# Expert weights in transfers of two slabs (2 MB, 16 KB runs), with the ring of 20 slabs handled as 10 groups

## The reference

```python
logits = t @ w_router + b_router              # 256 tokens, 32 experts, the best 4 of each token
up = xb @ w_up[e] + b_up[e]                   # w_up[e]: 1024 x 2048, 8 MB
glu, lin = up[:, :D_FF_EXPERT], up[:, D_FF_EXPERT:]
glu = jnp.minimum(glu, SWIGLU_LIMIT)
lin = jnp.clip(lin, -SWIGLU_LIMIT, SWIGLU_LIMIT)
act = glu * jax.nn.sigmoid(SWIGLU_ALPHA * glu) * (lin + 1)
y = act @ w_down[e] + b_down[e]               # w_down[e]: 1024 x 1024, 4 MB
```

## Time and profile before

| | |
|---|---|
| Time, median of 3 runs | 1238.82 us (1234.84 to 1239.2) |
| The profiled execution's own time | 1234.07 us |
| Its span, first to last instruction | 1232.4 us |
| PE busy | 1152.1 us, 93% of the span |
| DVE, ACT, POOL busy | 330.0, 237.0, 85.7 us |
| Data moved | 436.22 MB, mean 354 GB/s over the span |
| DMA packets | 65135 |

### The profile page before, as it was taken

One profiled execution on the slowest core, in us unless ns is written; L12 is line 12 of the kernel. 1 busy time (PEld: TensorE's weight loads), 2 busy tenths in 40 slices (PEclk: granted clock), 3 DMA queues, 4 the chain that ended last, 5 costly groups with the idle time before them and its releaser, 6 DMA issues.

```text
span 1232.4 us, 17087 instructions
## 1 busy us (share of the span) xinstructions
PE 1152.1 (93%) x5306; PEld 497.6 (40%) x5307; DVE 330.0 (27%) x859; ACT 237.0 (19%) x453; POOL 85.7 (7%) x204
## 2 busy tenths in 40 slices
PE   6969999998999999999899999999989999899996
PEld 5757548653333333333333333333333333333332
DVE  1389631333211122221111232111111111111112
ACT  2214121321121111112111121121111111111112
POOL 1098000010000000000000000000000000000000
PEclk9989999999999999999999999999999999999999
DMA  9230643909999999999999999999999999999991
GB/s 354 93 145 3 271 171 137 370 22 394 422 421 421 421 422 422 421 421 422 421 422 422 421 422 422 421 422 421 421 404 422 421 422 422 391 422 422 421 398 46
DMA packets 65135, 436.22 MB, mean 354 GB/s; under 512 B 8019, under 2 KB 8190, under 8 KB 15934
## 3 DMA queue, kind: packets, MB, share of 16 engines
q1 hardware_dynamic: 65086, 435.68, 85.7%
HBM read 434.61 MB, written 1.05 MB: 354 GB/s over the span
## 4 chain that ended last, share of the span: by engine, by line
PE 47%; SPq 36%; issue 6%; DMA 5%; DVE 3%; ACT 2%; ACTq 0%; DVEq 0%
SPq L390 22%; PE bank L1476 14%; SPq L394 11%; PE bank L1490 8%; DMA ring<-in_w_up_dram 5%; PE total L1449 2%; PE bank L1436 2%; PE bank L1188 2%; PE bank L1361 2%; PE bank L1210 2%; DVE ring L903 1%; SPq L429 1%; SPq L428 1%; PE bank L1201 1%; PE total L1400 1%
## 5 line engine op out<-in xcount | busy, mean ns | idle before, releaser
L1476 PE MATMUL bank<-ring,buf_m 128*64 128x512 f32 x2112 | 474.1, 597 | 40.3 <-DMA ring<-in_w_up_dram 38.5
L1476 PEld LDWEIGHTS bank<-ring,buf_m 128*64 128x64 f32 x2112 | 145.7, 137 | 362.6 <-issue 263.7
L1490 PE MATMUL bank<-ring,buf_m 128*64 128x512 f32 x1056 | 239.5, 595 | 0.0
L1111 DVE COPY buf_f<-bank 128x512 f32<-128x512 f32 x33 | 22.8, 692 | 589.9 <-PE bank L1476 589.9
L1490 PEld LDWEIGHTS bank<-ring,buf_m 128*64 128x64 f32 x1056 | 72.8, 136 | 137.6 <-issue 129.2
L759 ACT ACTIVATE buf_f<-bank 128x512 f32<-128x512 f32 x33 | 19.7, 597 | 403.3 <-PE bank L1476 403.3
L1449 PE MATMUL total<-buf_m,wr_sb 64*128 64x512 f32 x272 | 67.6, 615 | 0.8 <-ACT buf_m L771 0.8
L1436 PE MATMUL bank<-buf_k,buf_v 128*64 128x512 f32 x272 | 65.9, 605 | 0.7 <-DVE buf_v L1062 0.7
L539 POOL TENSOR_TENSOR buf_v<-table,buf_v 128x4 f32<-128x4 f32 x33 | 6.6, 199 | 804.0 <-DVE buf_v L1099 803.7
L1117 DVE TENSOR_TENSOR buf_f<-bank,buf_v 128x512 f32<-128x512 f32 x66 | 45.4, 687 | 59.5 <-PE bank L1510 59.5
L756 ACT ACT_TABLE_LOAD x33 | 42.3, 1283 | 33.7 <-issue 33.7
(11 more groups left out here) (327 smaller groups left out, 915.8 us busy)
## 6 DMA issues: line engine op xcount, KB each, us to landing
ring<-in_w_up_dram SPq DMA_DIRECT2D x256, 1024.0 KB, 26.2
ring<-in_w_down_dram SPq DMA_DIRECT2D x128, 1024.0 KB, 26.4
ring<-in_w_in_dram SPq DMA_DIRECT2D x4, 1440.0 KB, 10.8
ring<-in_w_xkv_dram SPq DMA_DIRECT2D x2, 2048.0 KB, 24.3
ring<-in_w_xkv_dram SPq DMA_DIRECT2D x1, 4096.0 KB, 13.4
ring<-in_w_out_dram SPq DMA_DIRECT2D x1, 4096.0 KB, 14.1
ring<-in_w_xq_dram SPq DMA_DIRECT2D x2, 2048.0 KB, 21.1
ring<-in_w_xo_dram SPq DMA_DIRECT2D x1, 4096.0 KB, 12.8
```

The source lines that it names most:

```text
L1476: ins = t_.matmul(banks[c][h * 64:(h + 1) * 64, :], xg[:, k, :], w[:, h * FF + c * BANK:h * FF + (c + 1) * BANK], start=k == 0, stop=k == ...
L1490: ins = t_.matmul(banks[2][h * 64:(h + 1) * 64, :], actT[:, f, :], slab(slot_of(at))[:, k * D + h * BANK:k * D + (h + 1) * BANK], start=f ...
```

## The change

Two slabs make a group (`GROUP = 2`); the ring is 10 groups, and an expert takes 6 loads of 2 MB (4 of `w_up`, 2 of `w_down`) instead of 12 of 1 MB. The host now lays out `w_up` too so that a partition's share of one expert, 64 KB, is one piece in DRAM; a load takes 16 KB of it on each partition. (The address of a partition's run so lies 64 KB behind that of the partition before, where it was 8 KB; for `w_down` it is 32 KB before and after, with runs of 16 KB in place of 8 KB.) There is one semaphore per group. TensorE waits once for each group and raises `up_steps` and `down_steps` after the second slab of each; SyncE waits for these, so that a slot pair is free when both its slabs are used. In the trunk slab 3 of expert 1 (issued with the down slabs at about 166 us) and slab 0 of expert 1 (issued after `xs11`) move behind `gffn`, where four slabs of expert 1 now go out in two loads. What TensorE computes, and in which order, is the same.

```diff
-RING, SLABS, CYCLE = 20, 12, 5
+GROUP = 2
+UPS, DOWNS = 8 // GROUP, 4 // GROUP
+RING, LOADS, CYCLE = 20 // GROUP, 12 // GROUP, 5
...
-        up_v = w_up[0].rearrange("e (k p) n -> e p k n", p=P)
+        up_v = w_up
...
+        def group(slot):
+            return slab(slot * GROUP, GROUP)
+
+        WIDE = GROUP * SLAB
...
-            def load_up(e, at, k):
-                slot = slot_of(at + k)
-                sp.dma_start(slab(slot), up_v[e, :, k, :]).then_inc(slab_in[slot], 16)
+            def load_up(e, at, i):
+                slot = slot_of(at + i)
+                sp.dma_start(group(slot), up_v[e, :, i * WIDE:(i + 1) * WIDE]).then_inc(group_in[slot], 16)
...
-            for i in range(4):
+            for i in range(DOWNS):
                 load_down(0, 0, i)
-            load_up(1, SLABS, 3)
...
-            for k in range(4, KT):
-                load_up(0, 0, k)
-            wait_drained(sp, "xs11")
-            load_up(1, SLABS, 0)
+            load_up(0, 0, 2)
+            load_up(0, 0, 3)
             wait_drained(sp, "xv3")
-            for k in range(4):
-                load_up(0, 0, k)
+            load_up(0, 0, 0)
+            load_up(0, 0, 1)
             wait_drained(sp, "xo3")
             sp.dma_start(gffn, g_ffn[0:1, :].broadcast_to([P, D])).then_inc(loaded["gffn"], 16)
-            load_up(1, SLABS, 1)
-            load_up(1, SLABS, 2)
+            load_up(1, LOADS, 0)
+            load_up(1, LOADS, 1)
...
-                    for k in range(4):
-                        sp.wait_ge(up_steps, n2 * KT + (k + 5))
-                        load_up(e, j * SLABS, k)
-                    for k in range(4, KT):
-                        sp.wait_ge(down_steps, n2 * 4 + (k - 3))
-                        load_up(e, j * SLABS, k)
+                    for i in range(DOWNS):
+                        sp.wait_ge(up_steps, n2 * UPS + (DOWNS + i + 1))
+                        load_up(e, j * LOADS, i)
+                    for i in range(DOWNS, UPS):
+                        sp.wait_ge(down_steps, n2 * DOWNS + (i - DOWNS + 1))
+                        load_up(e, j * LOADS, i)
                     n1 = last_block(e - 1)
-                    for i in range(4):
-                        sp.wait_ge(up_steps, n1 * KT + (i + 1))
-                        load_down(e, j * SLABS, i)
+                    for i in range(DOWNS):
+                        sp.wait_ge(up_steps, n1 * UPS + (i + 1))
+                        load_down(e, j * LOADS, i)
...
+            def wait_loaded(turn, at):
+
+                pe.wait_ge(group_in[slot_of(at)], turn * (CYCLE * LOADS // RING * 16) + (at // RING + 1) * 16)
+
             def up_slabs(n, turn, j):
 
                 for k in range(KT):
-                    at = j * SLABS + k
-                    pe.wait_ge(slab_in[slot_of(at)], turn * (CYCLE * SLABS // RING * 16) + (at // RING + 1) * 16)
-                    w = slab(slot_of(at))
+                    i, part = divmod(k, GROUP)
+                    at = j * LOADS + i
+                    if part == 0:
+                        wait_loaded(turn, at)
+                    w = group(slot_of(at))[:, part * SLAB:(part + 1) * SLAB]
...
-                    ins.then_inc(up_steps, 1)
+                    if part == GROUP - 1:
+                        ins.then_inc(up_steps, 1)
...
+    inputs["w_up"] = np.asarray(inputs["w_up"])[0].reshape(E, KT, P, 2 * FF).transpose(0, 2, 1, 3).reshape(E, P, KT * 2 * FF)
```

More of the change, by code:

```diff
@@ L306, in build_program @@
         table_ready = sem("ranks_and_gates_in_table")
-        slab_in = [sem(f"slab{i}_in") for i in range(RING)]
+        group_in = [sem(f"slabs{i * GROUP}_to_{i * GROUP + GROUP - 1}_in") for i in range(RING)]
         p2_ready = sem("onehot_for_gather_ready")
@@ L386, in _ @@
                 sp.dma_start(wxq_sb[:, 4 * i:4 * i + 4, :], w_xq_v[:, 4 * i:4 * i + 4, :]).then_inc(loaded[f"wxq{i}"], 16)
-            def load_up(e, at, k):
-                slot = slot_of(at + k)
-                sp.dma_start(slab(slot), up_v[e, :, k, :]).then_inc(slab_in[slot], 16)
+            def load_up(e, at, i):
+                slot = slot_of(at + i)
+                sp.dma_start(group(slot), up_v[e, :, i * WIDE:(i + 1) * WIDE]).then_inc(group_in[slot], 16)
             def load_down(e, at, i):
-                slot = slot_of(at + KT + i)
-                sp.dma_start(slab(slot), down_v[e, :, i * SLAB:(i + 1) * SLAB]).then_inc(slab_in[slot], 16)
+                slot = slot_of(at + UPS + i)
+                sp.dma_start(group(slot), down_v[e, :, i * WIDE:(i + 1) * WIDE]).then_inc(group_in[slot], 16)
             wait_drained(sp, "oT1")
             sp.wait_ge(yconv_ready, 1)
-            for i in range(4):
+            for i in range(DOWNS):
                 load_down(0, 0, i)
-            load_up(1, SLABS, 3)
             wait_drained(sp, "w11")
@@ L418, in _ @@
                 sp.dma_start(y_sb[h * 64:h * 64 + E, :], b_down[0, :, h * BANK:(h + 1) * BANK]).then_inc(loaded["bdown"], 16)
-            for k in range(4, KT):
-                load_up(1, SLABS, k)
+            load_up(1, LOADS, 2)
+            load_up(1, LOADS, 3)
             sp.wait_ge(rows_ready, TT)
@@ L432, in _ @@
             n1 = last_block(0)
-            for i in range(4):
-                sp.wait_ge(up_steps, n1 * KT + (i + 1))
-                load_down(1, SLABS, i)
+            for i in range(DOWNS):
+                sp.wait_ge(up_steps, n1 * UPS + (i + 1))
+                load_down(1, LOADS, i)
             with sp.Fori(0, (E - 2) // CYCLE) as turn:
@@ L756, in _ @@
                     a.activation(scrap[:, 3:4], eps[:, 0:1], ACT.Sigmoid)
-                    act.wait_ge(up_steps, b * KT + KT)
+                    act.wait_ge(up_steps, b * UPS + UPS)
                     a.activation(U_sb[:, 0:BANK], banks[0], ACT.Copy).then_inc(u_by_a, 1)
@@ L768, in _ @@
                     gathered_columns(b + 1, 0)
-                    act.wait_ge(down_steps, b * 4 + 4)
+                    act.wait_ge(down_steps, b * DOWNS + DOWNS)
                     act.wait_ge(pt_copied, b + 2)
@@ L1109, in _ @@
                     onehot_for_gather(b + 1)
-                    dve.wait_ge(up_steps, b * KT + KT)
+                    dve.wait_ge(up_steps, b * UPS + UPS)
                     v.tensor_copy(U_sb[:, BANK:2 * BANK], banks[1]).then_inc(u_by_v, 1)
@@ L1478, in up_slabs @@
                                             start=k == 0, stop=k == KT - 1)
-                    ins.then_inc(up_steps, 1)
+                    if part == GROUP - 1:
+                        ins.then_inc(up_steps, 1)
             def down_slabs(n, turn, j, half):
                 pe.wait_ge(act_ready, n * 2 + (half + 1))
[L1484 to L1493, removed]
+                for f in range(4 * half, 4 * half + 4):
+                    i, part = divmod(f, 2 * GROUP)
+                    at = j * LOADS + UPS + i
+                    if part == 0:
+                        wait_loaded(turn, at)
+                    for h in range(2):
+                        ins = t_.matmul(banks[2][h * 64:(h + 1) * 64, :], actT[:, f, :],
+                                        group(slot_of(at))[:, part * D + h * BANK:part * D + (h + 1) * BANK],
+                                        start=f == 0, stop=f == KT - 1)
+                    if part == 2 * GROUP - 1:
+                        ins.then_inc(down_steps, 1)
             def expert(e, turn, j):
```

## The result

The changed kernel takes 1209.16 us in the median of 4 runs (1207.0 to 1211.06), the kernel before beside it 1239.01. The ratio is 0.9764, with a 95% interval of 0.9734 to 0.9794: 2.4% faster, some 29 us. The profiled execution took 1207.0 us, its span 1205.3. The forecast was 1227, the range 1215 to 1243: the sign was right, the gain was more than twice as large. The page counts 37461 DMA packets in place of 65135, so the transfers are made of 16 KB packets as intended. One later execution of the changed kernel (in e12) took 1723.75 us at a granted clock of 0.654; it stands in no ratio and moves e12's median by 0.4 us.

The account below looks back on a forecast made before the run. The prediction took the stream of weight loads as the bound. Its terms, -11.5 - 3 + 1.8 + 1.7 = -11.0 us, gave 1223.1 against the profiled 1234.07 and 1227.8 on the median, stated as 1227, range 1215 to 1243.

Parts of the forecast that it names:

- late engine: At the stream's end, one DMA engine of 16 finishes some 15 us late, put down to instruction fetches.
- Fewer instructions on SP: SP's load loop: about half its load instructions go, one fetch less per turn, 3 us off the late engine (0 to 6).
- The packets: Expert loads after the restart: 16 KB runs save four packets per MB at 7.9 ns each, -11.5 us.
- The first refill: At the restart: a slot pair is free one slab of PE's work later, leaving a stream gap, +1.8 us.
- The last up load: Last expert: PE gets slabs 6 and 7 together, so two slabs of work remain, +1.74 us.
- A: Rival on the expert loads: the run length doesn't matter, 1239 to 1242 us; chance 0.32.
- B: Rival on the up loads: the new layout of `w_up`, runs 64 KB apart, reads slower, 1254 us; chance 0.09.
- C: Rival on SP's loop: instruction fetches become slower behind 16 KB packets, 1245 to 1251 us; chance 0.04.
- D: Rival on the expert loads: packets give more than 11.5 us (-17), fetches 6, so 1219 us; chance 0.06.

Follow-up runs that it names:

- e12: The changed kernel itself, unaltered, run again beside the version with split ends: 1207.6 us, ratio 0.9757 to the kernel before.
- e2: The changed kernel with SyncE's loop lengthened to 284 instructions a turn by table reads nobody uses: 1226.93 us, ratio 0.9911 to the kernel before.
- e10: The kernel before with SyncE's loop shortened to 245 instructions a turn, one wait for four slabs: 1226.26 us, ratio 0.9900.
- e1: The changed kernel with its 2 MB transfers made of 8 KB runs: 1222.4 us, ratio 0.9885 to the kernel before.
- e5: The changed kernel with its 2 MB transfers made of 4 KB runs: 1248.75 us, ratio 1.0100 to the kernel before.
- e9: The changed kernel with the first refill and the last up group of every fifth expert in halves: 1210.1 us, ratio 0.9767 to the kernel before.
- e8: The changed kernel with groups of four slabs, 4 MB transfers and 32 KB runs: 1212.91 us, ratio 0.9800 to the kernel before.
- e4: The changed kernel with each 2 MB group in one piece in DRAM: 1209.6 us, ratio 0.9771 to the kernel before.

## Why the prediction was wrong, by its own steps

The bound was read rightly: PE needs 26.71 us for a block, the loads give one in 29.85, and what the stream gained was passed on. So was the late engine: its tail comes and goes with the fetches (e2, e10).

**The step that failed is "Fewer instructions on SP".** It counted one fetch less per turn, 0.5 us each, 3 us in all. The runs show that this loop isn't fetched again after its first turn at 245 instructions or fewer, and that at 260 or more it is fetched anew in every turn: it isn't fewer fetches in proportion to fewer instructions, but all or none. 26 fetches went, not 6, and each cost 0.7 us, not 0.5. The 0.5 counted only the tail of 14 to 15 us. Before that, the other engines had twice run out of work at the end of SyncE's standstill at a turn, while one went on (a share of 0.08); in the kernel before:

```profile
896.00:900.00 4.00, 1.00 0.77 268
1047.00:1052.00 5.00, 1.00 0.59 216
1049.00:1050.00 1.00, 1.00 0.08 33
```

These are the dips to 404 and 391 of the earlier trace rows (the 398 holds the end of the stream). They are another 3 us, so the late engine was some 18 us behind, 0.7 for each of the 26 fetches. With that the term is -17.8 us (e2) and not -3; its bound of -6 was too narrow, since the count of 2 fetches less a turn that it took as the end assumed that the jump back always fetches. The row to ask was there: the 5 fetches in each turn, in which the loop body was the same every time.

**The packets** were the right mechanism and nearly the right size: -11.5 forecast, 364 x 0.038 = -13.8 by the windows, +13 in e1. The choice of the longest 4 KB stretch was the good one: its 411 GB/s is close to the 409 to 410 of a steady stream of such runs (e5). Why the windows of 5 and 9 us read 419 and 426 was not tried. The overhead of about 3 cycles per packet in the Trainium skill ("DMA: Bandwidth & Descriptors", "Why small descriptors are slow", with the 850 MHz of "Where 436 GB/s comes from") gave an estimate of 3.5 ns a packet, 5.1 us in all. The runs show 9 to 11 ns, and the measurement decides.

**The first refill** went out at 291.71, 5.02 us after PE began at 286.69; before it was 288.73 - 285.43 = 3.30. The difference of 1.72 us is the 1.74 forecast, and the gap is there too (share 0.50). That it costs 1.8 us is not shown: e9 filled part of this gap and another opened. **The last up load** shows in the rows as was said: after its landing PE has 3.65 us of work in place of 1.94. That this is worth 1.7 us of time is not shown either, since e9 took the wait away and the last up work ended no earlier.

**Sum.** From PE's first up matmul to the end of the span it was 1232.4 - 285.43 = 947.0 us and is 1205.3 - 286.69 = 918.6, a difference of -28.4. The parts are -13.8 for the packets and -17.8 for the fetches, both measured, and +1.7 for the last up load by its rows, -29.9 together. The 1.5 us left are of the size of the first refill's 1.8 and no larger than what separates two executions (918.6 to 920.3 in the table).

**The rivals.** A fell with e5, e1 and e8, which show the rate rising with every doubling of the run; B with e4; C with e2, which has both 16 KB packets and fetches: SyncE's queue stands still for 874.78 - 863.44 = 11.3 us at the turn, as it did for 11.0 before, and the plateau holds 428.

```profile
859.68 3.76 SPq L401 DMA_DIRECT2D ring<-in_w_down_dram  x2
874.78 10.01 SPq L397 DMA_DIRECT2D ring<-in_w_up_dram  x4
```

D's case for a gain beyond the forecast came true, but by the fetches, not the packets, and its 0.06 was too little for it.

## What to carry to other kernels

When a stream of loads sets the time, look at how it ends: one DMA engine that works on alone is a delay of that engine, and the instruction fetches of a loop that is fetched anew in every turn are enough for it, even if the loop's own engine has plenty of time. Here 15 instructions in a loop of some 250 decided over it. Longer runs save a price per packet, which a second kernel with another run length measures well. Larger groups bring a longer gap at the first refill and more work behind the last load, so the longest run wasn't the fastest kernel here.

## What the runs showed of the hardware that was not expected

- The loop on SyncE: at 194, 224 and 245 instructions a turn no fetch on q14 from the second turn on, at 260, 284 and 314 five in each turn from then on. A fetch of 8 KB cost the kernel about 0.7 us, more than twice what one of the weights' 8 KB packets takes of an engine's time at 421.5 GB/s (2.488/8 = 0.31 us). Where the rest of the 0.7 goes stays open.
- The price of a packet is the same from 4 KB to 32 KB, 9 to 11 ns.
- The expert loop began about 5 us later in the profiled executions of e2, e4, e8, e9 and e10 than in the others (starts above), with the same work of TensorE before it. That is about the spread of 4 us among runs of one kernel. In these five, and in none of the others, TensorE was granted 1.2 GHz once more in the trunk, for 10 us; e12 and e4 (PE busy and count, granted clock, DMA share, GB/s):

```profile
126.50:136.50 10.00, 10.00 (x49) 1.00 1.02 411
126.50:136.50 10.00, 10.00 (x35) 0.51 1.02 413
```

In the 16 us before, from 110 to 126, PE was busy for 15.00 us in e12 and for 14.99 in e4, both at 1.00. Why the clock fell in one execution and not in the other was not tried; it stays open.
